# One gather for both rows of a pick: an expert layer whose two tables lie side by side

## The chip, the cores and the metric

The kernel runs on one core of a Trainium2 chip. The core has a matrix engine (PE; its weight loads are listed apart as PEld), a vector engine (DVE), a scalar engine (ACT), a general engine (POOL) and a queue engine (SP); 16 DMA engines bring data from the chip's memory (HBM) into the core's own (the tensor `arena`, 128 partitions), and matrix products end in a small memory of eight banks (`ps`). The metric is the device time of one execution in microseconds (us), as the median of several; less is better. Everything is in float32.

## What is computed

One layer of a decoder, for 512 prompt tokens and 8 sample tokens of 1024 numbers: retention and attention heads, cross-attention, and then the part that the change is about, a product-key expert layer (PEER). For each token and each of 8 heads it picks 16 of 16,384 experts, so 128 picks a token. An expert is one row `u` and one row `v`, of 1024 numbers (4 KB) each:

```
idx = jnp.take_along_axis(cand_i, best_pos, axis=-1)          # 8 heads x 16 picks a token
g = jax.nn.softmax(best_s, axis=-1)
u = peer_u[idx]
a = jax.nn.gelu(jnp.einsum('nd,nhkd->nhk', xb, u), approximate=False)
v = peer_v[idx]
return jnp.einsum('nhk,nhkd->nd', g * a, v)
```

So `u` is wanted first (a dot product with the token), then gelu and the weight, and then `v` (times the weight, summed over the picks).

## The kernel before

The 512 prompt tokens are four blocks of 128, one token to a partition; the 8 sample tokens are a fifth block. The program is written out for each engine, and semaphores order the engines among each other.

**Gathers.** POOL issues all gathers of expert rows, in a loop over a block's picks (lines 508 to 533). One gather (L505) brings, for one pick number, one row for each of 128 tokens: 128 rows of 4 KB, 512 KB. Picks go in chunks of 8 (`CHUNK`): eight gathers of `u`, then eight of `v`. Each slot of `arena` has a semaphore for its landing (`u_in0` to `u_in7`, `v_in0` to `v_in7`), and a gather waits until its slot has been consumed: `u_used` counts the dot products, `v_used` the weighted sums.

**Block 0** has no stretch of its own. While the other blocks go through mixing, cross-attention and routing, its picks are fitted in between that work on DVE, as "half-steps" at 32 places (`PLACES`, lines 398 to 404): an even half-step is eight dot products (L1100), an odd one the weights and eight weighted sums (L1109). At most places there is one half-step. Only eight slots of 4 KB are free then (`VSLOT`); the other eight (`WSLOT`) hold weight matrices. So `u` and `v` of a chunk take turns in the same eight slots: the gathers of `v` start one by one as the dot products free the slots, and the next chunk's `u` as the weighted sums free them. Between two half-steps stands what the stage asks of DVE, often one residual addition (L1089, listed as L810, the line of the helper).

**Blocks 1 to 3** follow one after the other, with eight slots for `u` (`WSLOT`) and eight for `v` (`VSLOT`). For a chunk, DVE makes eight dot products (L1317), ACT the gelu of eight numbers (L776), DVE the eight weights (L1358; L1338 in block 1), ACT eight diagonal matrices of the weights (L780), and PE multiplies each with the slot of `v` and sums in `ps` (L1786). Between the chunks DVE selects the picks of the next block (`select_head`, lines 1139 to 1184). The gathers of block b + 1 wait on `sel_ready`, which DVE raises after the last head's selection (`gates`, line 1195); block 1's wait for each head's selection instead.

**The sample** comes last: eight gathers of `u`, eight of `v` (lines 535 to 540), one token each, with 128 picks on the partitions.

## Time and profile before

| | before |
|---|---|
| time, median of 3 runs | 2610.83 us (2597.9 to 2616.35) |
| the profiled execution: span, first to last instruction | 2647.7 us |
| PE / DVE / ACT / POOL busy | 73% / 59% / 14% / 47% |
| DMA over the whole span | 273 GB/s |
| gathers of expert rows (L505) | 520 of `peer_u`, 520 of `peer_v` |
| software-issued DMA (the gathers): share of 16 engines' span | 62.9% |
| HBM read | 713.11 MB |

The profiled execution's span is 36.9 us (1.4%) above the median of the unprofiled runs; no time of it other than its span is given. In the rows below, a timeline row gives start, duration, engine, line, operation, output and input, count, and in brackets how long the engine was idle before it and what ended that. A busy time by itself doesn't tell what limits a stage: one has to see which wait ends last there.

### The profile page before, as it was taken

Reading aid. Unit: us, or ns where it says so; the run is one execution under the profiler, and the core shown is the slowest. Engines: PE = TensorE matmul, PEld = TensorE weight load, DVE = VectorE, ACT = ScalarE, POOL = GpSimd, SP = SyncE. Lnnn points to the kernel's source line nnn. Section 1 sums busy time; section 2 is a strip of 40 time slices with the busy share of each in tenths; the row PEclk is TensorE's granted clock in tenths of the full one; section 3 lists DMA queues with packets and bytes.
Section 4 is the critical chain, followed back from the end, with each engine's and each line's share of the span. In section 5 each row is a group of like instructions: output and inputs, shape, how many; then the busy total and the mean of one; then the engine's idle time right before and its main releaser. Section 6 shows DMA issues by size and latency. Waiting matters only on the chain.

```text
span 2647.7 us, 19720 instructions
## 1 busy us (share of the span) xinstructions
PE 1938.7 (73%) x4940; PEld 856.2 (32%) x4940; DVE 1566.2 (59%) x3287; ACT 379.2 (14%) x859; POOL 1239.5 (47%) x1180
## 2 busy tenths in 40 slices
PE   5998798689876594478585667676767775667667
PEld 3334333522354133113352222232323232223222
DVE  1662367530148766977798667665655656555462
ACT  3012300000110012000200111111111112111111
POOL 0110001122001765457743777776777776777662
PEclk8999789599888897588897888887888887887886
DMA  6463034367442977788883999998999998999994
GB/s 266 172 253 115 32 120 162 131 250 255 167 141 103 359 288 315 246 340 309 302 301 115 362 358 346 369 361 326 359 368 358 364 367 315 359 367 354 354 347 159
DMA packets 207497, 723.91 MB, mean 273 GB/s; under 512 B 20009, under 2 KB 24873, under 8 KB 197073
## 3 DMA queue, kind: packets, MB, share of 16 engines
q0 software_dynamic: 159616, 614.54, 62.9%
q1 hardware_dynamic: 39632, 99.73, 10.3%
q10 hardware_dynamic: 8192, 8.95, 1.0%
q8 instruction: 28, 0.46, 0.1%
q14 instruction: 29, 0.23, 0.0%
HBM read 713.11 MB, written 10.03 MB: 273 GB/s over the span
## 4 chain that ended last, share of the span: by engine, by line
PE 30%; DVE 21%; issue 21%; POOL 14%; DMA 8%; ACT 3%; another core or an unknown queue 1%; POOLq 1%; DVEq 0%; ACTq 0%; SPq 0%
POOL arena L505 14%; PE ps L1435 11%; PE ps L1786 7%; DVE arena L810 5%; PE ps L1604 4%; DMA arena<-in_peer_u,arena 4%; DVE arena L1100 4%; DVE arena L1109 4%; DMA arena<-in_peer_v,arena 3%; DVE arena L1317 1%; PE ps L1398 1%; PE ps L1799 1%; DVE arena L1123 1%; DVE arena L1118 1%
## 5 line engine op out<-in xcount | busy, mean ns | idle before, releaser
L1786 PE MATMUL ps<-arena 128*128 128x512 f32 x1536 | 781.1, 672 | 361.0 <-ACT arena L780 208.5
L505 POOL DMA_INDIRECT arena<-in_peer_u,arena x520 | 581.3, 1118 | 284.5 <-issue 156.4
L505 POOL DMA_INDIRECT arena<-in_peer_v,arena x520 | 571.4, 1099 | 255.9 <-issue 144.2
L1317 DVE CUSTOM_DVE_ANT_0 arena<-arena 128x1024 f32<-128x1024 f32 x384 | 468.8, 1226 | 325.0 <-DMA arena<-in_peer_u,arena 292.4
L1786 PEld LDWEIGHTS ps<-arena 128*128 128x128 f32 x1536 | 328.2, 217 | 814.6 <-issue 580.2
L1435 PE MATMUL ps<-arena 128*128 128x512 f32 (+1 forms) x1168 | 534.7, 616 | 18.5 <-DVE arena L810 12.9
L1435 PEld LDWEIGHTS ps<-arena 128*128 128x128 f32 (+1 forms) x1168 | 205.2, 179 | 336.8 <-issue 334.5
L496 POOL DMA_INDIRECT arena<-in_cache_diff_k,arena x32 | 30.1, 941 | 421.4 <-DVE arena L873 366.5
L1109 DVE SCALAR_TENSOR_TENSOR arena<-arena 128x1024 f32<-128x1024 f32 x128 | 164.5, 1285 | 35.6 <-DMA arena<-in_peer_v,arena 26.1
L810 DVE TENSOR_TENSOR arena<-arena 128x256 f32<-128x256 f32 (+10 forms) x353 | 131.2, 396 | 77.4 <-remote 23.9
L810 DVE TENSOR_TENSOR arena<-arena,ps 128x2048 f32<-128x2048 f32 (+3 forms) x78 | 118.3, 1522 | 84.7 <-PE ps L1435 34.3
L1100 DVE CUSTOM_DVE_ANT_0 arena<-arena 128x1024 f32<-128x1024 f32 x128 | 151.5, 1225 | 19.6 <-DMA arena<-in_peer_u,arena 17.6
L1759 PE MATMUL ps<-arena 128*128 128x128 f32 (+1 forms) x512 | 132.1, 418 | 1.5 <-DVE arena L1278 0.8
L776 ACT ACTIVATE arena<-arena 128x8 f32<-128x8 f32 x48 | 10.1, 210 | 844.1 <-DVE arena L1317 567.1
L517 POOL COPY arena<-arena 128x8 uint32 x64 | 16.8, 262 | 237.9 <-DVE arena L810 201.4
L780 ACT ACTIVATE arena<-arena 128x128 f32<-128x128 f32 x384 | 117.4, 388 | 58.2 <-DVE arena L810 26.5
L810 DVE TENSOR_TENSOR arena<-ps,arena 128x512 f32<-128x512 f32 (+3 forms) x44 | 35.4, 827 | 148.1 <-PE ps L1607 104.9
L1604 PE MATMUL ps<-arena 128*8 128x512 f32 x256 | 111.9, 592 | 3.9 <-DMA arena<-in_cache_diff_v,arena 3.9
L1398 PE MATMUL ps<-arena 128*128 128x128 f32 (+1 forms) x256 | 41.1, 322 | 92.6 <-DVE arena L819 80.3
L1759 PEld LDWEIGHTS ps<-arena 128*128 128x128 f32 x512 | 86.9, 215 | 40.3 <-issue 9.1
L496 POOL DMA_INDIRECT arena<-in_cache_diff_v,arena x32 | 33.8, 1055 | 123.3 <-PE ps L1604 114.4
L580 ACT ACTIVATE arena<-ps 128x512 f32<-128x512 f32 (+1 forms) x43 | 25.6, 596 | 349.0 <-PE ps L1435 342.6
(227 smaller groups left out, 1437.9 us busy)
## 6 DMA issues: line engine op xcount, KB each, us to landing
arena<-in_w_pq SPq DMA_DIRECT2D x8, 2048.0 KB, 12.1
arena<-in_w_in SPq DMA_DIRECT2D x7, 2048.0 KB, 10.0
arena<-in_peer_u,arena POOLq DMA_INDIRECT x520
arena<-in_peer_v,arena POOLq DMA_INDIRECT x520
arena<-in_w_out SPq DMA_DIRECT2D x4, 2048.0 KB, 8.3
arena<-in_w_mq SPq DMA_DIRECT2D x4, 2048.0 KB, 16.0
arena<-in_w_mo SPq DMA_DIRECT2D x4, 2048.0 KB, 13.2
arena<-in_cache_mem_k SPq DMA_DIRECT2D x8, 1024.0 KB, 4.9
```

The source lines that it names most:

```text
L496: pool.indirect_dma_start(SLOT[n % RING], None, k_rows if kind == "k" else v_rows, bass.IndirectOffsetOnAxis(kv_idx[:, b * GRP + g:b * GRP ...
L505: return pool.indirect_dma_start(slot, None, table[0], bass.IndirectOffsetOnAxis(idx.bitcast(U32), 0))
L780: act.activation(DIAG[k], ident, ACT.Copy, scale=WCH[:, k:k + 1]).then_inc(s["diag_ready"], 1)
L810: return dve.tensor_tensor(out, a, b, op)
L1100: dve.tensor_tensor_reduce(VSLOT[k], VSLOT[k], QR[:, 0, :], 1.0, 0.0, ALU.mult, ALU.add, dots[:, k:k + 1]).then_inc(s["u_used"], 1)
L1109: dve.scalar_tensor_tensor(out=HR[:, 0, :], in0=VSLOT[k], scalar=WCH[:, k:k + 1], in1=HR[:, 0, :], op0=ALU.mult, op1=ALU.add).then_inc(s[" ...
L1317: dve.tensor_tensor_reduce(WSLOT[k], WSLOT[k], QR[:, blk, :], 1.0, 0.0, ALU.mult, ALU.add, dots[:, k:k + 1]).then_inc(s["u_used"], 1)
L1398: last = pe.transpose(tb[:, P * k:P * k + r], c, ident[0:r, 0:r])
L1435: last = pe.matmul(PS[0:r, PSUM_JOB + j % 2, :], xt[:, k, P * u:P * u + r], W[t % 2][:, k, :], start=(k == 0), stop=(k == KD - 1))
L1604: last = pe.matmul(PS[0:HC, 4 + b % 2, :], S[:, c0:c0 + HC], SLOT[n % RING][:, 512 * j:512 * j + 512], start=(g == 0 and j == 0), stop=False)
L1759: last = pe.matmul(PS[:, 4 + x % 2, 0:tokens], W[t % 2][:, k, P * (x % 4):P * (x % 4) + P], XT[:, k, first:first + tokens], start=(k == 0) ...
L1786: last = pe.matmul(PS[:, bank + i, :], DIAG[k], VSLOT[k][:, 512 * i:512 * i + 512], start=False, stop=False, skip_group_check=True)
```

## The change

The two tables arrive as one, `peer_uv`, whose row is an expert's `u` followed by its `v` (8 KB). The joining is done once on the host and is no part of the device time. One gather of 128 rows of 8 KB brings both rows of a pick, and a slot is 8 KB: four slots (`UV0`) while block 0 runs, in the same 32 KB a partition that the eight slots took, and eight (`UV`) from block 1 on, in the same 64 KB. A slot is free again only when its `v` half has been used, so every gather waits on `v_used`. 

In block 0 a batch is four picks. Each place has twice as many half-steps as before: where there was one (eight dot products, or eight weighted sums) there are now both halves of one batch: four dot products, gelu, weights, four weighted sums. In blocks 1 to 3 dot products, gelu, weights and diagonals go in pairs of picks (`PAIR`): DVE makes the dot products of pair q, then the weights of pair q - 1. The region `misc` is moved to the front of the layout so that a slot of 8 KB fits across two neighbouring regions.

```diff
-CHUNK = 8
+UV0 = 4
+UV = 8
+PAIR = 2
...
-        VSLOT = ([at("const", CO["rot"][0] + 1024 * i, 1024) for i in range(3)] + [at("xtm", 1024 * i, 1024) for i in range(2)]
-                 + [at("dvs", 0, 1024)] + [at("ring", 4096 + 1024 * i, 1024) for i in range(2)])
-        WSLOT = [at("w", 1024 * i, 1024) for i in range(CHUNK)]
+        UVSLOT = ([at("const", CO["rot"][0] + NB * NSEL + 2048 * i, 2048) for i in range(2)] + [at("xtm", 0, 2048), at("ring", 4096, 2048)]
+                  + [at("w", 2048 * i, 2048) for i in range(UV - UV0)])
+        USLOT, VSLOT = [x[:, 0:D] for x in UVSLOT], [x[:, D:2 * D] for x in UVSLOT]
...
         def half_steps_at(place):
-            before = sum(n for i, (p, n) in enumerate(PLACES) if i < [q for q, _ in PLACES].index(place))
-            return range(before, before + dict(PLACES)[place])
+            before = 2 * sum(n for i, (p, n) in enumerate(PLACES) if i < [q for q, _ in PLACES].index(place))
+            return range(before, before + 2 * dict(PLACES)[place])
...
-                        for k in range(CHUNK):
-
-                            pool.wait_ge(s["u_used"] if blk else s["v_used"], c2 * (2 * CHUNK) + (done + k + 1))
+                        for k in range(UV):
+
+                            pool.wait_ge(s["v_used"], c2 * (2 * UV) + free_count(blk, UV * half + k))
                             pool.nop(nofuse=True)
-                            gather(uslot[k], peer_u, ICH[half][:, k:k + 1]).then_inc(uv_in[0][k], 16)
-                        for k in range(CHUNK):
-
-                            if blk:
-                                pool.wait_ge(s["v_used"], c2 * (2 * CHUNK) + (done + k + 1))
-                            else:
-                                pool.wait_ge(s["u_used"], c2 * (2 * CHUNK) + (done + CHUNK + k + 1))
-                            pool.nop(nofuse=True)
-                            gather(VSLOT[k], peer_v, ICH[half][:, k:k + 1]).then_inc(uv_in[1][k], 16)
+                            slot = k if blk else k % UV0
+                            gather(UVSLOT[slot], ICH[half][:, k:k + 1]).then_inc(uv_in[slot], 16)
...
+            def turn_of_slots(blk, c):
+                for q in range(UV // PAIR):
+                    ks = range(PAIR * q, PAIR * q + PAIR)
+                    act.wait_ge(s["u_used"], c * UV + dotted(blk, ks[-1]))
+                    act.activation(gl[:, ks[0]:ks[-1] + 1], dots[:, ks[0]:ks[-1] + 1], ACT.Gelu).then_inc(s["gelu_done"], 1)
+                    act.wait_ge(s["weight_ready"], c * (UV // PAIR) + (NBATCH + NSEL // PAIR * (blk - 1) + q + 1))
+                    for k in ks:
+                        act.wait_ge(s["v_used"], c * UV + free_count(blk, k))
+                        act.activation(DIAG[k], ident, ACT.Copy, scale=WCH[:, k:k + 1]).then_inc(s["diag_ready"], 1)
...
-                        for k in range(CHUNK):
-                            dve.wait_ge(uv_in[1][k], 16 * (c + 1))
-                            dve.wait_ge(s["v_used"], CHUNK * (c + 1) + k)
+                        for k in range(UV0):
+                            dve.wait_ge(s["v_used"], UV0 * (c + 1) + k)
                             dve.scalar_tensor_tensor(out=HR[:, 0, :], in0=VSLOT[k], scalar=WCH[:, k:k + 1], in1=HR[:, 0, :],
                                                      op0=ALU.mult, op1=ALU.add).then_inc(s["v_used"], 1)
...
-            def weights_wanted(blk, c, h2):
-                dve.wait_ge(s["gelu_done"], h2 * 2 + (NCH * blk + c + 1))
-                dve.wait_ge(s["v_used"], h2 * (2 * CHUNK) + CHUNK * (NCH * blk + c + 1))
+            def weights_wanted(blk, half, h, q):
+                dve.wait_ge(s["gelu_done"], h * (2 * UV // PAIR) + (NBATCH + NSEL // PAIR * (blk - 1) + UV // PAIR * half + q + 1))
+
+
+            def picks(blk, half, h, weigh):
+
+                for q in range(UV // PAIR):
+                    dot_products(blk, half, h, q)
+                    if q:
+                        weigh(half, q - 1)
+                weigh(half, UV // PAIR - 1)
...
+    inputs["peer_uv"] = np.concatenate([np.asarray(inputs.pop(name)) for name in ("peer_u", "peer_v")], axis=2)
```

Where the instructions stand. First DVE in block 0, at the first two places (the mixing stage's residual additions are the rows with `job_ready`). Before, from the last dot product of one place to the first weighted sums of the next:

```order
L1100 ISA arena<-arena 128x1024 [waits u_in7]
L1100 ISA arena 128x1
L810 TENSOR_TENSOR arena<-arena,ps 128x512 [waits job_ready]
L810 TENSOR_TENSOR arena<-arena,ps 8x512 [waits job_ready]
L810 TENSOR_TENSOR arena<-arena 128x8 [waits gelu_done]
L1109 SCALAR_TENSOR_TENSOR arena<-arena 128x1024 [waits v_used,v_in0,weight_ready]
L1109 SCALAR_TENSOR_TENSOR arena<-arena 128x1024 [waits v_used,v_in1]
```

and now, from the last dot product of a batch to the first of the next batch:

```order
L1104 ISA arena<-arena 128x1024 [waits uv_in3]
L1104 ISA arena 128x1
L814 TENSOR_TENSOR arena<-arena 128x4 [waits gelu_done]
L1112 SCALAR_TENSOR_TENSOR arena<-arena 128x1024 [waits v_used,weight_ready]
L1112 SCALAR_TENSOR_TENSOR arena<-arena 128x1024 [waits v_used] x3
L814 TENSOR_TENSOR arena<-arena,ps 128x512 [waits job_ready]
L814 TENSOR_TENSOR arena<-arena,ps 8x512 [waits job_ready]
L1104 ISA arena<-arena 128x1024 [waits uv_in0]
```

The residual additions stood between the dot products and the weighted sums of a chunk; now they stand between two batches, and the weights follow the dot products at once.

Second POOL, at the turn from one chunk to the next in block 0. Before:

```order
L517 COPY arena<-arena 128x8
L519 REGISTER_ALU
L505 DMA arena<-in_peer_u,arena 128x1024 [waits idx_copied,v_used]
L505 DMA arena<-in_peer_u,arena 128x1024 [waits v_used] x7
L531 REGISTER_ALU
L505 DMA arena<-in_peer_v,arena 128x1024 [waits u_used]
```

and now:

```order
L530 COPY arena<-arena 128x8
L532 REGISTER_ALU
L535 REGISTER_ALU [waits idx_copied]
L519 DMA arena<-in_peer_uv,arena 128x2048 [waits v_used]
L535 REGISTER_ALU
```

The gathers of `v`, which waited for dot products, are gone, and each gather that is left brings twice the bytes and waits for a weighted sum.

Third DVE in the loop of blocks 2 and 3. Before, the end of one chunk and the start of the next:

```order
L1317 ISA arena<-arena 128x1024 [waits u_in7]
L1317 ISA arena 128x1
L1321 ISA
L1322 ISA [waits gelu_done]
L810 ISA [waits v_used]
L810 TENSOR_TENSOR arena<-arena 128x8
L1316 REGISTER_ALU
L1317 ISA arena<-arena 128x1024 [waits u_in0]
```

and now, the end of a turn of eight slots and the start of the next:

```order
L1319 ISA arena<-arena 128x1024 [waits uv_in7]
L1319 ISA arena 128x1
L1323 REGISTER_ALU
L814 ISA [waits gelu_done]
L814 TENSOR_TENSOR arena<-arena 128x2
L1323 REGISTER_ALU
L814 ISA [waits gelu_done]
L814 TENSOR_TENSOR arena<-arena 128x2
```

The wait on `v_used` ahead of the weights is gone; two weight instructions, of the last two pairs, follow the last dot product.

## Rows read from the trace of the kernel before

**Rows 1.** Stages: start:end, us, busy by engine, PEclk, DMA share, GB/s

```profile
851.00:1421.00 570.00, 404.19 (x1119) 184.40 (x1119) 439.84 (x763) 63.07 (x127) 333.59 (x272) 0.81 0.81 297
1444.00:1823.00 379.00, 251.75 (x495) 106.09 (x496) 255.91 (x626) 66.57 (x176) 276.17 (x272) 0.81 0.95 354
1823.00:2198.00 375.00, 266.92 (x518) 111.80 (x517) 219.74 (x514) 64.59 (x162) 273.04 (x272) 0.82 0.96 358
2198.00:2590.00 392.00, 266.10 (x536) 112.06 (x534) 225.07 (x533) 69.54 (x170) 271.42 (x271) 0.83 0.93 344
```

**Rows 2.** DVE's groups from 851 to 1421 us: count, busy us, mean ns

```profile
L1109 DVE SCALAR_TENSOR_TENSOR arena<-arena 128x1024 f32<-128x1024 f32 x128 | 164.5, 1285 | 35.6 <-DMA arena<-in_peer_v,arena 26.1 <-DVE arena L1109 0.5
L1100 DVE CUSTOM_DVE_ANT_0 arena<-arena 128x1024 f32<-128x1024 f32 x128 | 151.5, 1225 | 19.6 <-DMA arena<-in_peer_u,arena 17.6 <-ACT arena L563 1.1
```

**Rows 3.** DVE's timeline in block 0, four neighbouring half-steps

```profile
1210.73 11.01 DVE L1109 SCALAR_TENSOR_TENSOR arena<-arena 128x1024 f32<-128x1024 f32 x8
1221.66 0.68 DVE L810 TENSOR_TENSOR arena<-arena,ps 128x512 f32<-128x512 f32 x1
1222.26 1.22 DVE L1100 CUSTOM_DVE_ANT_0 arena<-arena 128x1024 f32<-128x1024 f32 x1
...
1231.42 1.27 DVE L810 TENSOR_TENSOR arena<-arena,ps 128x512 f32<-128x512 f32 x2
```

**Rows 4.** DVE's timeline, the end of a long gap before weighted sums

```profile
1035.48 0.18 DVE L1227 RECIPROCAL arena<-arena 128x4 f32<-128x4 f32 x1 [8.84 <-PE ps L1672]
...
1037.03 1.28 DVE L1109 SCALAR_TENSOR_TENSOR arena<-arena 128x1024 f32<-128x1024 f32 x1
```

**Rows 5.** POOL's timeline at those half-steps: gathers, and what ended the wait

```profile
1212.79 1.45 POOL L505 DMA_INDIRECT arena<-in_peer_u,arena  x1 [7.92 <-DVE arena L1109]
...
1226.88 1.99 POOL L505 DMA_INDIRECT arena<-in_peer_v,arena  x1 [0.31 <-issue]
```

**Rows 6.** The first gather of block 0 (POOL), and its first dot product (DVE)

```profile
852.33 0.96 POOL L505 DMA_INDIRECT arena<-in_peer_u,arena  x1 [0.87 <-POOL arena L517]
...
856.69 1.23 DVE L1100 CUSTOM_DVE_ANT_0 arena<-arena 128x1024 f32<-128x1024 f32 x1 [4.48 <-DMA arena<-in_peer_u,arena]
```

**Rows 7.** Timeline in block 2: gelu after the last dot product, weights

```profile
2003.30 0.21 ACT L776 ACTIVATE arena<-arena 128x8 f32<-128x8 f32 x1 [15.77 <-DVE arena L1317]
2003.74 0.60 DVE L810 TENSOR_TENSOR arena<-arena 128x8 f32<-128x8 f32 x2 [0.48 <-issue]
```

**Rows 8.** SP's queue of weights and memory rows, 851 to 1421 us: packets, MB, share

```profile
q1 hardware_dynamic: 10912, 34.60, 16.1%
```

**Rows 9.** Gather queue, 4 KB rows, 2250 to 2500 us

```profile
q0 software_dynamic: 24830, 90.43, 97.0%
```

**Rows 10.** Gather queue, 8 KB rows of the paged cache, 555 to 600 us

```profile
q0 software_dynamic: 1546, 11.29, 64.9%
```

**Rows 11.** The same gathers, 500 to 650 us

```profile
q0 software_dynamic: 4208, 30.02, 55.3%
```

**Rows 12.** Block 1's end: DVE's last weights, then POOL's next gather

```profile
1813.78 0.23 DVE L1338 SCALAR_TENSOR_TENSOR arena<-arena 128x8 f32<-128x8 f32 x1 [4.02 <-remote]
...
1823.54 0.96 POOL L505 DMA_INDIRECT arena<-in_peer_u,arena  x1 [0.86 <-POOL arena L517]
```

**Rows 13.** Block 3's end: DVE's last dot product, then POOL's sample gather

```profile
2569.31 1.23 DVE L1317 CUSTOM_DVE_ANT_0 arena<-arena 128x1024 f32<-128x1024 f32 x1
...
2590.43 0.94 POOL L505 DMA_INDIRECT arena<-in_peer_u,arena  x1 [15.36 <-DVE arena L1374]
```

**Rows 14.** Stretches at the three block ends, and one in block 0

```profile
1815.00:1826.00 11.00, 11.00 (x22) 4.57 (x22) 9.97 (x49) 4.44 (x9) 2.46 (x4) 0.82 0.33 109
2194.00:2206.00 12.00, 12.00 (x29) 5.34 (x28) 10.93 (x60) 1.59 (x2) 5.84 (x8) 0.98 0.62 217
2574.00:2592.00 18.00, 13.79 (x33) 5.87 (x32) 10.30 (x27) 7.57 (x11) 2.20 (x3) 0.96 0.47 189
1246.00:1250.00 4.00, 0.26 (x1) 0.00 (x0) 2.53 (x3) 0.00 (x0) 3.39 (x3) 0.88 1.02 408
```

More of the change, by code:

```diff
@@ L501, in _, with gather @@
                                    state_ret[0, b].rearrange("h d e -> d h e")).then_inc(tile_in[n % RING], 16)
-            def gather(slot, table, idx):
-                return pool.indirect_dma_start(slot, None, table[0], bass.IndirectOffsetOnAxis(idx.bitcast(U32), 0))
+            def gather(slot, idx):
+                return pool.indirect_dma_start(slot, None, peer_uv[0], bass.IndirectOffsetOnAxis(idx.bitcast(U32), 0))
             for blk in range(NBLK):
@@ L691, in peer_half_steps @@
                     if n % 2:
-                        act.wait_ge(s["u_used"], CHUNK * (n // 2 + 2))
-                        act.activation(gl, dots, ACT.Gelu).then_inc(s["gelu_done"], 1)
+                        act.wait_ge(s["u_used"], dotted(0, UV0 * (n // 2) + UV0 - 1))
+                        act.activation(gl[:, 0:UV0], dots[:, 0:UV0], ACT.Gelu).then_inc(s["gelu_done"], 1)
             def keep_sample_scores(x):
@@ L771, in _ @@
                     gate_exp(0)
-            def chunk(blk, c):
-                act.wait_ge(s["u_used"], c * CHUNK + CHUNK * (NCH * blk + 2))
-                act.activation(gl, dots, ACT.Gelu).then_inc(s["gelu_done"], 1)
-                act.wait_ge(s["weight_ready"], c + (NCH * blk + 1))
-                for k in range(CHUNK):
-                    act.wait_ge(s["v_used"], c * CHUNK + (CHUNK * NCH * blk + k + 1))
-                    act.activation(DIAG[k], ident, ACT.Copy, scale=WCH[:, k:k + 1]).then_inc(s["diag_ready"], 1)
+            def turn_of_slots(blk, c):
[7 more added lines that the diff above has]
+                        act.activation(DIAG[k], ident, ACT.Copy, scale=WCH[:, k:k + 1]).then_inc(s["diag_ready"], 1)
             with act.Fori(0, PH) as h:
@@ L785, in _ @@
                 for half in range(2):
-                    chunk(1, h * 2 + half)
+                    turn_of_slots(1, h * 2 + half)
             gate_exp(2)
             for blk in range(2, NBLK):
-                with act.Fori(0, NCH) as c:
-                    chunk(blk, c)
+                with act.Fori(0, NTURN) as c:
+                    turn_of_slots(blk, c)
                 gate_exp(blk + 1)
@@ L1333, in head_of_block_1, with weigh @@
                 dve.nop(nofuse=True)
-                for half in range(2):
-                    if half:
-                        dot_products(1, 1, h)
-                    weights_wanted(1, half, h)
-                    dve.scalar_tensor_tensor(out=WCH, in0=GE[:, CHUNK * half:CHUNK * half + CHUNK], scalar=rgate, in1=gl,
-                                             op0=ALU.mult, op1=ALU.mult).then_inc(s["weight_ready"], 1)
-                    if half == 0 and not last:
-                        select_head(1, 1, h + 1)
+                def weigh(half, q):
+                    weights_wanted(1, half, h, q)
+                    dve.scalar_tensor_tensor(out=WCH[:, PAIR * q:PAIR * q + PAIR], in0=GE[:, UV * half + PAIR * q:UV * half + PAIR * q + PAIR],
+                                             scalar=rgate, in1=gl[:, PAIR * q:PAIR * q + PAIR], op0=ALU.mult, op1=ALU.mult
+                                             ).then_inc(s["weight_ready"], 1)
+                picks(1, 0, h, weigh)
+                if not last:
+                    select_head(1, 1, h + 1)
+                picks(1, 1, h, weigh)
                 select_head(2, 2, h)
@@ L1354, in _, with weigh @@
                 with dve.Fori(0, PH) as h:
-                    for half in range(NCH // PH):
-                        dot_products(blk, half, h)
-                        weights_wanted(blk, half, h)
-                        tt(WCH, gl, GATE[:, blk, bass.ds(h * (2 * CHUNK) + half * CHUNK, CHUNK)], ALU.mult).then_inc(s["weight_ready"], 1)
+                    def weigh(half, q):
+                        weights_wanted(blk, half, h, q)
+                        tt(WCH[:, PAIR * q:PAIR * q + PAIR], gl[:, PAIR * q:PAIR * q + PAIR],
+                           GATE[:, blk, bass.ds(h * (2 * UV) + half * UV + PAIR * q, PAIR)], ALU.mult).then_inc(s["weight_ready"], 1)
+                    for half in range(2):
+                        picks(blk, half, h, weigh)
                     select_head(blk + 1, blk + 1, h)
@@ L1780, in _ @@
                 open_group(bank, P)
[L1781 to L1784 removed]
+                with pe.Fori(0, NTURN) as c:
+                    for k in range(UV):
+                        pe.wait_ge(s["diag_ready"], c * UV + (NSEL * (blk - 1) + k + 1))
                         for i in range(2):
@@ L1801, in _ @@
                 last.then_inc(s["xb_ready"], 1)
[L1802 removed]
+            pe.wait_ge(s["u_used"], dotted(NBLK, DB - 1))
             open_group(6, DB)
```

90 lines of the change are left out of this document (41 added, 49 removed).

## The prediction, made before the changed kernel was run

> **What bounds the kernel now.** I read the stages first [rows 1]. In blocks 1 to 3 the DMA engines are busy 0.93 to 0.96 of the time and no engine more than 0.73: these 1146 us are bound by the gathers. Block 1's 379 us less 7.4 us idle at its end [rows 14] make 2.90 us for each of 128 picks, 1.05 MB at about 362 GB/s, as in [rows 9].
>
> Block 0's stage (851 to 1421 us) is different. DVE is the busiest (440 of 570 us), DMA has 0.81 [rows 1]. DVE's groups say what it does: 164.5 us of weighted sums and 151.5 us of dot products, and it waits only 26.1 and 17.6 us for their rows [rows 2]. The timeline shows why so little: eight weighted sums take 11.0 us without a stop, 0.6 us of other work, then the dot products run at once [rows 3], because the gather of the next `u` began at 1212.79, right after the first weighted sum had freed its slot [rows 5]. Consuming and loading overlap over a whole half-step. From the same timeline I took the 31 gaps between the 32 half-steps, from the end of one to the start of the next (two are in [rows 3], 0.6 and 1.3 us; a long one ends in [rows 4]). 19 are under 7 us, 32 us together; 12 are 7.8 to 32 us, 167 us together.
>
> **Block 0: the loads come out from under the work.** A batch is now four picks; pick j waits for the weighted sum of pick j - 4, and weighted sums are the last thing in a batch. So during the dot products, gelu and weights nothing is loading. From the end of a batch's first weighted sum:
> - the gather starts 0.8 us later (1212.0 to 1212.79) [rows 3, 5];
> - its rows are in 4.4 us after that (852.33 to 856.69) for 512 KB [rows 6], and the second 512 KB add 1.4 us at 362 GB/s;
> - the other three picks follow at 2.9 us each: 8.7 us.
>
> So the fourth pick is in after 15.3 us. The other three weighted sums take 4.1 us (1.38 each [rows 3]), so this is 11.2 us after the batch's end. The dot products alone would reach the fourth 3.5 us after they start (1.15 each: eight in 1222.26 to 1231.42 [rows 3]). A gap g thus leaves a wait of 7.7 us - g. The 19 short gaps cost 19 x 7.7 - 32 = 114 us, the long ones nothing. (One round of a tight run then takes 18 to 19 us, where a half-step and its gap now take about 12.)
>
> Second, gelu and weights now stand inside the batch: gelu starts at 2003.30, the weights end at 2003.91, and the next work starts about 0.2 us later, 0.85 us in all [rows 7]. 32 times this, less the 16 weight instructions of 0.2 us that the gaps held: +24 us.
>
> Third, the 44 us of waits that DVE has now [rows 2] are replaced by these: -44 us.
>
> Fourth, the chain was costed with free DMA engines, but SP moves 34.6 MB in this stage [rows 8], 95 us at that rate. Between nothing and 95 x 19/31 = 58 us of it falls into exposed loads; I take the middle, +30.
>
> Fifth, some gaps are waits for PE or ACT (8.84 us in [rows 4]) that were started before the batch ahead of them; a longer batch uses them up. Three such gaps follow a lengthened batch (5 to 6 us each), and at one place dot products can go ahead of a late gelu: between 0 and -35 us, I take -20.
>
> Sum for block 0: 114 + 24 - 44 + 30 - 20 = +104; I take **+100**, between +40 (all ends in its favour, and a chain 1 us shorter) and +150.
>
> The gathers in this stage become fewer, and under running dot products one takes 1.99 us instead of 0.96 [rows 5, 6]. That is no gain here: POOL mostly waits for DVE.
>
> **Blocks 1 to 3: the ends.** The last eight `v` of a block, 11.6 us of DMA, stream in while DVE already does the last weights, the selection and `gates`; only then may the next gather start. So DMA now idles only 7.4, 4.6 and 9.5 us at the three ends (the missing part of the DMA share in the first three of [rows 14]). With `u` and `v` together, the last dot product comes after the last byte. At block 1's end the weights start at 1813.78, after 4.0 us on `v_used` that fall away, and the next gather at 1823.54: 9.8 us [rows 12]. To this come 1.2 us of dot product, about 1.8 us for the weights of the last two pairs and the diagonals between them (gelu 0.85 us as above), and about 2.8 us from gather to data and from landing to DVE (between nothing and the 2.9 us that [rows 6] leave beside the transfer): 15.6 us. Twice this, and for the third end 2570.5 to 2590.43 [rows 13] + 1.3 + 1.2 + 2.8 = 25 us, are 56 us against 21.5: **+35** (27 to 45).
>
> **Blocks 1 to 3: the rate.** Between the ends the gathers bound the time before and, I expect, after. Eight slots of 8 KB hold as much as sixteen of 4 KB. A slot is held while its pair is dotted, the next pair lands and is dotted (5.8 us), then 0.85 us, two diagonals and two products of PE, some 12 us; the round of eight is 23.2 us, and a refill takes 0.8 + 5.8 us. It fits, with about 5 us to spare. What remains is how fast rows of 8 KB go. With 4 KB the queue moves 90.43 MB in 0.970 of 250 us: 373 GB/s while busy [rows 9]. The trace has 8 KB rows too, in the gathers of the paged cache: 387 in a dense stretch [rows 10], 362 in a looser one [rows 11]. For 1114 us these are -40 and +34 us. The dense stretch is nearer to this use, but it shares the engines with SP's queue; I take **-15**.
>
> The Trainium skill ("DMA: Bandwidth & Descriptors", section "Anatomy of one DMA") fits a software-issued DMA as 2.0 us plus bytes at 436 GB/s, so 512 KB would take 3.2 us and 1 MB 4.4 us, an estimate by that page. If gathers went one at a time, a pick would fall from 6.4 to 4.4 us, and the sum would be hundreds of us lower. The trace disagrees with that use of it: two gathers pass in 2.90 us, less than one would take, so the fixed part is already overlapped.
>
> **The sample.** The first pair of rows is in 1.4 us later; after that PE's broadcasts set the pace as before: **+1.5**. Half of POOL's gathers fall away and buy nothing there: POOL is busy 0.73 of blocks 1 to 3 [rows 1], and runs ahead of the DMA engines. The smaller gelus and weights there cost ACT and DVE under 1 us a pair, beside 5.8 us of DMA.
>
> **Sum.** 100 + 35 - 15 + 1.5 = +121.5 us on the profiled 2647.7 us, or 4.6%. The median is 2610.83 us, so I scale by 0.986: +120, **2731 us**.
>
> **Rivals.**
> - *A, not slower: one read of 8 KB goes at the rate that the queue shows only at its best.* 408 GB/s stands in [rows 14] (1246 to 1250 us). If 8 KB rows kept that, 396 with the present 0.97 share, blocks 1 to 3 would lose 96 us, and four picks of block 0 would be in 1.1 us earlier, 19 times: 100 - 21 + 35 - 96 + 1.5 = +20, 2630 us. For: the dense stretch is above 373. Against: [rows 11]. It decides from about 395 GB/s on. 12%. The Trainium skill's page on DMA points this way in its section "Measured": its rates rise with a DMA's size, 341 GB/s at 1 MB and 425 at 16 MB.
> - *B, slower still: the slots starve the DMA queue in blocks 1 to 3.* The spare 5 us must cover a selection (most of the 9.8 us in [rows 12], some 7 us), in which DVE dots nothing. If each of the 31 selections (15 in block 1, 8 each after) left DMA idle for 2 us: +62, 2792 us. For: a slot now returns only through PE. Against: weights and diagonals of the last pair are out before the selection starts, so all eight slots fill during it. 15%.
> - *C: block 0 hides most of it.* If the stage's length is set by PE and ACT more than DVE's gaps show, block 0 costs +40: 2672 us. For: DVE idles 130 of 570 us [rows 1], and 86 of these are not for expert rows. Against: the short gaps hold residual additions of 0.7 us, with nothing behind them. 20%.
>
> My forecast has 53%. For it alone I would say 2690 to 2775 us. 2640 to 2800 us also takes in most of B and C and leaves out the better part of A and the far end of B. About 1% (26 us) is what can be told from no change: faster by more than that 3% (A at its best), within it 9% (the rest of A, a little of C), slower 88%.
>
> **What would show it.** In the changed profile: (1) block 0's stage some 100 us longer, its dot products waiting for `peer_uv` about 120 to 150 us in all where 17.6 us stood, the weighted sums waiting for no rows, and a DMA share near 0.7. (2) Gaps of 15 and 25 us without DMA at the three block ends. (3) Stretches inside blocks 2 and 3 at 0.96 or more DMA share and 355 to 375 GB/s; over 390 is A, a share under 0.93 is B. (4) POOL's busy time halved. If (1) fails, the chain of 15.3 us is wrong, most likely its 4.4 us, which was taken once, or the gaps are not DVE's own.

## The result, and the profile after

The changed kernel takes **2736.3 us** (median of four, 2728.4 to 2740.0) against 2607.8 us of the kernel before (2597.9 to 2616.4): a ratio of **1.0485, 95% interval 1.046 to 1.0509**. It is slower, and the predicted 2731 us is 5 us away. Where single executions of a kernel below were disturbed (3004 and 3290 us, in two kernels), they are left out of its median.

The stages of the changed kernel, as in [rows 1]: after the stretch and its length come the busy us of PE, PEld, DVE, ACT and POOL, PE's granted clock as a share of full speed, the DMA share and GB/s (here block 0's stage runs up to the first gather of block 1):

```profile
851.00:1549.00 698.00, 427.59 (x1139) 194.67 (x1139) 468.17 (x896) 68.52 (x148) 141.33 (x145) 0.76 0.63 242
1549.00:1923.00 374.00, 264.23 (x516) 109.42 (x516) 257.27 (x679) 76.81 (x226) 143.63 (x145) 0.84 0.90 359
1923.00:2292.00 369.00, 261.34 (x512) 107.90 (x512) 219.61 (x559) 74.34 (x210) 142.39 (x144) 0.85 0.91 364
2292.00:2669.00 377.00, 269.20 (x518) 110.58 (x518) 225.70 (x582) 79.27 (x218) 143.77 (x143) 0.84 0.90 358
```

Block 0 grew and its DMA share fell to 0.63. Blocks 1 to 3 seem to be 26 us shorter than in [rows 1], yet at a DMA share of only 0.90. That comparison misleads: the profiled execution of before was 40 us above its median. A second profile of the kernel before (the first experiment) is the better base. From first gather to first gather on POOL's timeline, in us:

| stage | before, first profile | before, second profile | after | after against the second |
|---|---|---|---|---|
| up to block 0's first gather | 852.3 | 860.0 | 852.0 | -8.0 |
| block 0 | 591.9 | 591.3 | 697.8 | **+106.5** |
| blocks 1, 2, 3 | 379.3, 375.0, 391.9 | 365.1, 361.2, 375.1 | 373.2, 369.7, 376.7 | **+18.2** |
| sample and end | 57.3 | 57.8 | 57.2 | -0.6 |

The first stage is not touched by the change and lies between 852 and 865 us in all the profiles here. From block 0's first gather on, the change costs 124 us; the sum predicted 121.5.

**Block 0.** DVE's waits in its stage (total, times, longest), to be read beside [rows 2]:

```profile
DVE arena L1104 <- DMA arena<-in_peer_uv,arena: 141.9, 79, 5.9
DVE arena L1230 <- PE ps L1687: 20.5, 3, 9.7
DVE arena L1119 <- PE ps L1764: 13.1, 9, 2.4
...
DVE arena L814 <- ACT arena L695: 8.7, 32, 0.3
```

The dot products wait 141.9 us for rows; the weighted sums (L1112) wait for none, as their group's row shows (after the last bar, 4.6 us of idle time, with no row among its causes):

```profile
L1112 DVE SCALAR_TENSOR_TENSOR arena<-arena 128x1024 f32<-128x1024 f32 x128 | 164.5, 1285 | 4.6
```

Before it was 17.6 + 26.1. One tight round, DVE first and then POOL:

```profile
1239.91 5.25 DVE L1112 SCALAR_TENSOR_TENSOR arena<-arena 128x1024 f32<-128x1024 f32 x4
1245.07 2.33 DVE L814 TENSOR_TENSOR arena<-ps,arena 4x1024 f32<-4x1024 f32 x2
1248.11 1.23 DVE L1104 CUSTOM_DVE_ANT_0 arena<-arena 128x1024 f32<-128x1024 f32 x1 [0.70 <-DMA arena<-in_peer_uv,arena]
...
1251.62 1.23 DVE L1104 CUSTOM_DVE_ANT_0 arena<-arena 128x1024 f32<-128x1024 f32 x1 [2.28 <-DMA arena<-in_peer_uv,arena]
...
1256.60 1.23 DVE L1104 CUSTOM_DVE_ANT_0 arena<-arena 128x1024 f32<-128x1024 f32 x1 [1.25 <-DMA arena<-in_peer_uv,arena]
...
1258.11 0.17 DVE L814 TENSOR_TENSOR arena<-arena 128x4 f32<-128x4 f32 x1 [0.27 <-ACT arena L695]
1258.31 5.25 DVE L1112 SCALAR_TENSOR_TENSOR arena<-arena 128x1024 f32<-128x1024 f32 x4
```

```profile
1241.97 1.38 POOL L519 DMA_INDIRECT arena<-in_peer_uv,arena  x1 [12.63 <-DVE arena L1112]
```

The first weighted sum ends at about 1241.2 (a quarter of 5.25 us). The gather follows 0.8 us later, its rows are dotted at 1248.11, the fourth pick's at 1256.60, 15.4 us after that first weighted sum. From weighted sums to weighted sums it is 18.4 us. The chain of 15.3 us and the round of 18 to 19 us of the prediction stand here row by row. It is not one lucky round: in 16 of the 31 the fourth dot product starts 14.9 to 15.8 us after the first weighted sum's end, in the others later, and the ten batches behind a gap of 8.7 us or more wait for no row.

**Blocks 1 to 3.** Cut at the block ends: three long stretches and the three ends of the changed kernel, then the same of the second profile of before.

```profile
1550.00:1906.00 356.00, 249.36 (x484) 103.33 (x485) 244.97 (x634) 70.73 (x213) 143.21 (x143) 0.83 0.94 373
1906.00:1928.00 22.00, 14.87 (x33) 6.08 (x31) 16.99 (x76) 5.14 (x11) 3.97 (x6) 0.89 0.31 117
1928.00:2276.00 348.00, 249.38 (x486) 103.13 (x487) 203.87 (x492) 69.20 (x199) 138.42 (x139) 0.84 0.95 380
2276.00:2298.00 22.00, 15.35 (x32) 5.74 (x30) 16.74 (x72) 5.14 (x11) 4.31 (x6) 0.92 0.28 102
2298.00:2645.00 347.00, 254.19 (x487) 104.94 (x488) 204.87 (x506) 69.98 (x202) 139.64 (x139) 0.84 0.96 382
2645.00:2670.00 25.00, 12.44 (x29) 5.16 (x28) 15.09 (x42) 9.29 (x16) 0.60 (x1) 0.83 0.15 63
```

```profile
1452.00:1804.00 352.00, 246.04 (x480) 103.11 (x480) 247.45 (x591) 60.06 (x164) 267.06 (x267) 0.82 0.99 371
1804.00:1820.00 16.00, 12.61 (x24) 5.43 (x25) 14.40 (x64) 5.53 (x12) 7.46 (x8) 0.73 0.69 267
1820.00:2170.00 350.00, 248.34 (x497) 104.41 (x496) 210.81 (x466) 61.68 (x159) 264.66 (x268) 0.86 0.99 377
2170.00:2182.00 12.00, 12.00 (x28) 5.33 (x27) 10.59 (x51) 2.92 (x4) 3.80 (x6) 0.96 0.59 213
2182.00:2530.00 348.00, 248.49 (x488) 104.08 (x486) 206.44 (x464) 59.06 (x150) 262.29 (x263) 0.83 0.99 372
2530.00:2556.00 26.00, 20.54 (x39) 8.72 (x40) 14.94 (x41) 10.47 (x20) 8.50 (x9) 0.82 0.61 226
```

Three things can be worked out (second last column: DMA share, last: GB/s).
- *Ends.* Without DMA: 0.69 x 22 + 0.72 x 22 + 0.85 x 25 = 52 us, against 0.31 x 16 + 0.41 x 12 + 0.39 x 26 = 20 us: **+32**.
- *Idle inside.* 0.06 x 356 + 0.05 x 348 + 0.04 x 347 = 53 us, against 0.01 x 1050 = 10 us: **+42**.
- *Rate while busy.* 373/0.94 = 397, 400 and 398 GB/s, against 375, 381 and 376. 384 picks of 1.049 MB are 403 MB; at 398 instead of 377 GB/s: **-57**.

The sum is +17, where +18.2 was measured. So a faster row was paid back almost in full by a queue that runs dry. Where it does is seen in block 2 after a selection. Windows, then PE and POOL:

```profile
2064.00:2068.00 4.00, 2.53 (x6) 0.76 (x4) 3.18 (x9) 0.00 (x0) 2.43 (x3) 1.00 1.00 422
2068.00:2072.00 4.00, 0.00 (x0) 0.00 (x0) 4.00 (x7) 0.21 (x1) 0.73 (x2) 0.89 1.01 426
2072.00:2076.00 4.00, 3.23 (x4) 1.51 (x5) 2.65 (x8) 0.79 (x3) 0.00 (x0) 0.50 1.01 422
2076.00:2078.00 2.00, 2.00 (x3) 0.67 (x2) 0.89 (x1) 0.79 (x3) 0.67 (x1) 0.51 0.83 344
2078.00:2080.00 2.00, 2.00 (x6) 0.95 (x5) 0.76 (x3) 0.00 (x0) 1.37 (x2) 1.00 0.35 82
```

```profile
2059.38 7.15 PE L1800 MATMUL ps<-arena 128*128 128x512 f32 x16 [0.51 <-ACT arena L784]
2072.77 13.56 PE L1800 MATMUL ps<-arena 128*128 128x512 f32 x25 [6.24 <-ACT arena L784]
```

```profile
2067.31 0.94 POOL L519 DMA_INDIRECT arena<-in_peer_uv,arena  x1 [0.79 <-PE ps L1800]
2068.24 0.49 POOL L530 COPY arena<-arena 128x8 uint32 x1
2077.33 1.84 POOL L519 DMA_INDIRECT arena<-in_peer_uv,arena  x1 [8.60 <-PE ps L1800]
```

During the selection (until 2067 us) DVE makes no weights, and the first pair's come only behind the second pair's dot products. ACT has no diagonals to make, PE nothing to do for 6.24 us, and then its granted clock is 0.50 (the level of 1.2 GHz) until 2078. The four products that free the first slot then start 0.85 us apart, at the full clock 0.43, so of the 8.6 us that POOL waits some 1.7 are the clock's (an estimate from those starts). POOL waits for a slot from 2068.7 to 2077.3, the gathers under way run out, and between 2078 and 2080 the DMA share is 0.35.

### The profile page after: what moved, and what is told of

Same layout as the page of the kernel before. It is cut to its first block, busy times and chain, and to the rows that moved or that the text cites. A ratio compares the mean times of both kernels' runs of the same rounds, so it can differ in the third digit from the quotient of the medians.

```text
span 2726.6 us, 19130 instructions
## 1 busy us (share of the span) xinstructions
PE 1963.2 (72%) x4940; PEld 859.0 (32%) x4940; DVE 1576.0 (58%) x3447; ACT 412.4 (15%) x1021; POOL 648.9 (24%) x660
## 4 chain that ended last, share of the span: by engine, by line
PE 39%; DMA 22%; DVE 21%; issue 12%; ACT 3%; POOL 3%; DVEq 1%; POOLq 0%; ACTq 0%; SPq 0%
DMA arena<-in_peer_uv,arena 20%; PE ps L1450 13%; PE ps L1800 12%; DVE arena L814 4%; PE ps L1619 4%; DVE arena L1319 3%; DVE arena L1104 3%; POOL arena L519 2%; PE ps L1774 2%; DVE arena L1112 2%; ACT arena L784 1%; PE ps L1764 1%; DVE arena L1181 1%; PE ps L1813 1%; PE ps L1687 1%
## 5 line engine op out<-in xcount | busy, mean ns | idle before, releaser
L1800 PE MATMUL ps<-arena 128*128 128x512 f32 x1536 | 789.4, 675 | 313.2 <-ACT arena L784 313.1
L519 POOL DMA_INDIRECT arena<-in_peer_uv,arena x520 | 557.3, 1072 | 1161.7 <-PE ps L1800 558.1
L1450 PEld LDWEIGHTS ps<-arena 128*128 128x128 f32 (+1 forms) x1168 | 206.0, 180 | 358.7 <-issue 356.0
L1104 DVE CUSTOM_DVE_ANT_0 arena<-arena 128x1024 f32<-128x1024 f32 x128 | 154.1, 1223 | 143.0 <-DMA arena<-in_peer_uv,arena 141.9
L784 ACT ACTIVATE arena<-arena 128x128 f32<-128x128 f32 x384 | 133.2, 394 | 548.5 <-DVE arena L814 353.5
L814 DVE TENSOR_TENSOR arena<-arena 128x256 f32<-128x256 f32 (+11 forms) x465 | 148.9, 339 | 57.3 <-ACT arena L780 33.3
L1112 DVE SCALAR_TENSOR_TENSOR arena<-arena 128x1024 f32<-128x1024 f32 x128 | 164.5, 1285 | 4.6
L1413 PEld LDWEIGHTS ps<-arena 128*128 128x128 f32 (+1 forms) x256 | 35.8, 178 | 158.1 <-DVE arena L823 83.4
L695 ACT ACTIVATE arena<-arena 128x4 f32<-128x4 f32 x32 | 6.6, 207 | 494.9 <-DVE arena L1104 494.9
L780 ACT ACTIVATE arena<-arena 128x2 f32<-128x2 f32 x192 | 37.0, 193 | 281.2 <-DVE arena L1319 281.2
```

What stands on the lines that cost most here:

```text
L519: return pool.indirect_dma_start(slot, None, peer_uv[0], bass.IndirectOffsetOnAxis(idx.bitcast(U32), 0))
L780: act.activation(gl[:, ks[0]:ks[-1] + 1], dots[:, ks[0]:ks[-1] + 1], ACT.Gelu).then_inc(s["gelu_done"], 1)
L784: act.activation(DIAG[k], ident, ACT.Copy, scale=WCH[:, k:k + 1]).then_inc(s["diag_ready"], 1)
L814: return dve.tensor_tensor(out, a, b, op)
L1104: dve.tensor_tensor_reduce(USLOT[k], USLOT[k], QR[:, 0, :], 1.0, 0.0, ALU.mult, ALU.add, dots[:, k:k + 1]).then_inc(s["u_used"], 1)
L1112: dve.scalar_tensor_tensor(out=HR[:, 0, :], in0=VSLOT[k], scalar=WCH[:, k:k + 1], in1=HR[:, 0, :], op0=ALU.mult, op1=ALU.add).then_inc(s[" ...
```

## The experiments

### Which base: the kernel before, profiled again (e8_before_again)

Expected: 

> The kernel before, unchanged, for a second profile of it: the first had a span of 2647.7 us, 40 us above its own median of 2606. If that execution was only an unlucky one, this span is about 2604 us, and the 40 us are missing in blocks 1 to 3 (first gather to first gather 379, 375, 392 us then, in sum 1146), which come to about 1105 us in sum, while block 0 stays at 592 us. Rival: the profiled execution always carries about 40 us more, spread over all stages; then the span is about 2645 us again.

Measured: span 2610.5 us, time 2612.4. Block 0 591.3 us, blocks 1 to 3 1101.4 us. The 45 us were missing in blocks 1 to 3 alone, as the first expectation had it. Inside the blocks the gathers moved 362 GB/s at a share of 0.97 in the first profile [rows 9], and 371 to 377 at 0.99 in the second (above). Why one execution's gathers were slower is open.

### Block 0 as it was (e1_block0_4k)

```diff
+        HSLOT = [UVSLOT[k // 2][:, D * (k % 2):D * (k % 2) + D] for k in range(UV)]
...
+                        if blk == 0:
+                            for table, used in ((peer_u, s["v_used"]), (peer_v, s["u_used"])):
+                                for k in range(UV):
+                                    pool.wait_ge(used, c2 * (2 * UV) + (UV * half + k + 1))
+                                    pool.nop(nofuse=True)
+                                    gather(HSLOT[k], ICH[half][:, k:k + 1], table).then_inc(uv_in[k], 16)
+                            continue
```

Expected: 

> The changed kernel, but block 0 as it was before: eight slots of 4 KB, eight gathers of u and eight of v in turns (from the two separate tables), half-steps of eight. Blocks 1 to 3 and the sample keep the 8 KB rows. Theory (in block 0 the loads come out from under the work): the loss sits in block 0 alone, so the stage from its first gather to block 1's first gather falls back from 698 to about 592 us and the time from 2736 to 2580 to 2630 us, not slower than the kernel before (2608). Rival (8 KB rows, pairs or the block ends cost it): block 0 gives back less than 50 us and the time stays above 2680.

Measured: 2627.4 us, ratio 1.0086 (1.0061 to 1.0112). Block 0 is back at 591.2 us, as expected, and blocks 1 to 3 stay at 1121 us; but the kernel is still 0.9% slower than the one before, which I had not expected. Of the 128 us that the change costs, 109 lie in block 0; what it does elsewhere costs the remaining 20 us.

### Batches of two (e2_batch2)

```diff
-                        for k in range(UV0):
-                            dve.wait_ge(uv_in[k], 16 * (c + 1))
...
+                    for k0 in range(0, UV0, SUB):
+                        for k in range(k0, k0 + SUB):
+                            dot(k)
+                        weigh_and_add(k0)
```

Expected: 

> The changed kernel with batches of two picks instead of four in block 0; same four slots, same gathers, same bytes. Theory (the chain from a freed slot to landed rows is exposed because all four slots are freed at the end of a batch): while one pair is worked on the other two slots load. From the end of a pair's first weighted sum its rows are in after 0.8 + 4.4 + 1.4 = 6.6 us and 9.5 us, and DVE comes back to them after 7.0 and 8.2 us, so about 1.3 us of wait is left for a pair. The dot products' wait for peer_uv falls from 142 us to 45 to 70 us, 32 more gelus and weights cost 15 us, time 2640 to 2690 us. Rival (the rows of 8 KB or the shared DMA engines limit block 0): same bytes, so the wait stays near 140 us and the time rises to about 2750.

Measured: 2694.3 us, ratio 1.0345 (1.0297 to 1.0393). DVE's waits in block 0:

```profile
DVE arena L1109 <- DMA arena<-in_peer_uv,arena: 52.6, 32, 5.9
DVE arena L817 <- ACT arena L698: 28.8, 64, 6.6
DVE arena L1131 <- PE ps L1776: 28.5, 9, 4.2
```

The same rows into the same slots, and the wait for them falls from 141.9 to 52.6 us. So most of that wait is neither the rows' size nor the shared engines, it is the batch that frees all slots at once. The time is 4 us above the expected range, because part came back: 20 us at gelu, and 15 us more at L1131, the router's top-16, which waits for PE's scores.

### A chain of single picks (e5_pipe)

```diff
...
+                    dot(0)
+                    for k in range(UV0):
+                        if k + 1 < UV0:
+                            dot(k + 1)
+                        weigh_and_add(k)
```

Expected: 

> The changed kernel with block 0's batches of four picks worked on in a chain of single picks: the dot product of pick k + 1 goes ahead of gelu, weight and weighted sum of pick k, so gelu is hidden behind a dot product and each slot is freed as soon as its pick is done. Same slots, gathers and bytes. Theory (exposed load chain plus inline gelu): after batches of two, 52.6 us of waits for rows and 28.8 us for gelu are left in block 0's stage (653 us). The gelu wait goes to nearly nothing, and a slot's refill (0.8 + 4.4 + 1.4 = 6.6 us) now has two dot products, two weights and two weighted sums (5.5 us) in front of it, so the wait for rows falls to 15 to 35 us; 64 more weights cost 13 us, and as with batches of two some 15 us come back as waits for PE: stage 605 to 630 us, time 2645 to 2675 us. Rival (what is left in block 0 is PE's and the shared DMA engines' time): the stage stays above 640 us and the time above 2680.

Measured: 2682.8 us, ratio 1.0272 (1.024 to 1.0305); block 0's stage 644.2 us. My expectation (stage 605 to 630 us, time 2645 to 2675) missed, and the rival's numbers came in. The gelu wait halved, but the wait for rows did not fall any more:

```profile
DVE arena L1109 <- DMA arena<-in_peer_uv,arena: 54.3, 40, 6.2
DVE arena L1132 <- PE ps L1777: 30.5, 9, 4.5
...
DVE arena L817 <- ACT arena L698: 14.1, 5, 6.6
```

What is left of this wait can be read gather by gather. Two gathers on POOL, and then the dot products of the same two picks:

```profile
1259.24 1.43 POOL L521 DMA_INDIRECT arena<-in_peer_uv,arena  x1 [2.55 <-DVE arena L1120]
1260.98 3.17 POOL L521 DMA_INDIRECT arena<-in_peer_uv,arena  x1 [0.30 <-issue]
```

```profile
1268.63 1.23 DVE L1109 CUSTOM_DVE_ANT_0 arena<-arena 128x1024 f32<-128x1024 f32 x1 [3.81 <-DMA arena<-in_peer_uv,arena]
1271.42 1.23 DVE L1109 CUSTOM_DVE_ANT_0 arena<-arena 128x1024 f32<-128x1024 f32 x1 [0.16 <-DMA arena<-in_peer_uv,arena]
```

The second gather takes 3.17 us, while DVE runs dot products and weighted sums without a stop, but its dot product waits only 0.16 us. The long wait, 3.81 us, is for the first gather: it began on time, 0.8 us after its slot came free, and its rows came 9.4 us later, while SP's queue was moving weights. Over the whole of block 0, the 81 gathers without traffic of SP's queue between issue and landing took 6.1 us (median), the 47 with it 8.7 us, and two thirds of DVE's waits for rows are for the latter. So most of what is left falls beside SP's transfers, as the rival had it; that they cause it is not shown, as no run here takes them away. The 30.5 us of waiting for PE could be followed too, and it is not PE's own time:

### The order on ACT (e11_act_order)

The waits of PE in the router's loop of the changed kernel, and then of this one:

```profile
PE ps L1764 <- ACT arena L766: 32.3, 6, 13.0
```

```profile
PE ps L1766 <- ACT arena L766: 16.4, 4, 12.3
```

In the changed kernel ACT's gelu of a batch (L695) stands ahead of its copy of the next router product (L766). One of the six places, ACT and then PE:

```profile
1426.40 0.21 ACT L695 ACTIVATE arena<-arena 128x4 f32<-128x4 f32 x1 [15.98 <-DVE arena L1104]
1426.51 0.47 ACT L766 COPY arena<-ps 128x392 f32<-128x392 f32 x1
```

```profile
1427.03 2.18 PE L1764 MATMUL ps<-arena 128*128 128x128 f32 x8 [3.87 <-ACT arena L766]
```

ACT stands 15.98 us until the batch's last dot product is done, the copy starts only behind the gelu, and PE stands 3.87 us for the copy.

```diff
-                    peer_half_steps(g, ("router", x))
+                    if x:
+                        peer_half_steps(g, ("router", x - 1))
+                peer_half_steps(g, ("router", NSUB - 1))
```

Expected: 

> The changed kernel with that edit alone (ACT's copy of the next router product ahead of the gelu of a batch). Theory: DVE's 13.1 us of waits for PE's router scores go and PE's 32.3 us of waits for ACT in the router's loop with them; block 0's stage 685 to 690 us instead of 698, time 2722 to 2730 us instead of 2736. Rival: no change, 2733 to 2740 us, the wait for PE's scores at 13 us as before.

Measured: 2719.9 us, ratio 1.0426 (1.0391 to 1.046), block 0's stage 688.0 us; 2 us below the expected range. DVE's wait for the router's scores falls from 13.1 to 1.2 us, while the wait for rows stays at 143.7 us. PE's wait for ACT, which was to go, fell only by half; 12.3 of the 16.4 us left are in the loop's first place. So 10 of block 0's 106 us (16 in the median) came from ACT's queue, which the prediction did not look at.

### Two gathers of 4 KB rows into a slot (e4_two_4k)

```diff
-                            gather(UVSLOT[slot], ICH[half][:, k:k + 1]).then_inc(uv_in[slot], 16)
+                            if blk:
+                                gather(USLOT[k], ICH[half][:, k:k + 1], peer_u).then_inc(uv_in[k], 16)
+                                gather(VSLOT[k], ICH[half][:, k:k + 1], peer_v).then_inc(uv_in[k], 16)
+                            else:
+                                gather(UVSLOT[slot], ICH[half][:, k:k + 1]).then_inc(uv_in[slot], 16)
```

Expected: 

> The changed kernel, but in blocks 1 to 3 a pick's two rows come by two gathers of 4 KB rows (from the two separate tables) into the two halves of the same slot; slots, pairs, waits and order stay. Theory (a row of 8 KB goes faster): while busy the queue falls from 403 to the 373 GB/s of before; with the same stalls that is 40 to 90 us over 384 picks, time 2775 to 2825 us. Rival (row size doesn't matter, and the higher rate comes from elsewhere): 2720 to 2750 us with 400 GB/s while busy.

Measured: 2800.1 us, ratio 1.0758 (1.0707 to 1.0808), 64 us above the changed kernel, all of it in blocks 1 to 3 (402, 386 and 399 us). The gather queue (packets, MB, share of 250 us), changed kernel from 2000 us and this one from 2030 us:

```profile
q0 software_dynamic: 13082, 95.25, 94.5%
```

```profile
q0 software_dynamic: 24837, 90.44, 96.7%
```

95.25 MB in 0.945 of 250 us are 403 GB/s while busy; 90.44 in 0.967 are 374. Slots, pairs and order are the same. The row's size differs, and with it the bytes of a gather (two of 512 KB for one of 1 MB) and the tables, two for one; these are not told apart in blocks 1 to 3 (in block 0, 4 KB rows from two tables or out of the joined one made no difference, e7 and e10 below). The gain from one gather of 8 KB rows is real, and larger than I had it. (The Trainium skill, "DMA: Bandwidth & Descriptors", section "Measured", gives rates that rise with a DMA's size; the direction agrees here, 374 GB/s for gathers of 512 KB and 403 for those of 1 MB, though both are above its 341 for 1 MB.)

### The selection in four parts (e3_split_select)

```diff
-                        picks(blk, half, h, weigh)
-                    select_head(blk + 1, blk + 1, h)
+                        picks(blk, half, h, weigh, () if half else select_parts(blk + 1, blk + 1, h))
...
                     dot_products(blk, half, h, q)
                     if q:
                         weigh(half, q - 1)
+                    next(parts, None)
```

Expected: 

> The changed kernel with each head's selection in blocks 1 to 3 cut into four parts, one behind each pair of picks, instead of in one piece of about 8 us between two turns; all else as it is. Theory S (during a selection PE runs out of weights, frees no slot for some 6 us and comes back at half its clock, so the DMA queue runs dry for about 3 us behind each of 31 selections): these gaps go, and at the three block ends the last selection no longer stands between the last dot product and the next gather (7.5 us each); blocks 1 to 3 lose 80 to 130 us, time 2610 to 2660 us, with a DMA share of 0.97 and more and over 390 GB/s inside the blocks. Rival (the gathers themselves go no faster than the 381 GB/s seen inside block 2): only the block ends are gained, 22 us, time 2714.

Measured: 2678.7 us, ratio 1.0296 (1.0229 to 1.0362). Block 2's inner stretch and its end:

```profile
1920.00:2248.00 328.00, 241.73 (x480) 98.30 (x480) 209.09 (x518) 68.56 (x197) 140.19 (x140) 0.89 0.99 400
2248.00:2267.00 19.00, 18.68 (x36) 7.78 (x36) 11.21 (x41) 5.79 (x14) 3.02 (x4) 0.83 0.42 160
```

The DMA share inside is 0.99, the rate 400 GB/s and more: the cause is the right one. The size was too high, and the time missed the expected range by 19 us. The idle inside was 53 us, not 31 x 3, and the ends gained 14 us (52 to 38), not 22. The cut takes away the late weights and PE's slow return together, so this run does not tell them apart.

### The same cut in the kernel before (e9_before_split)

The same four parts, one behind each second dot product of a chunk, in the kernel before.

Expected: 

> The kernel before (4 KB rows, separate u and v slots) with the same cut of each selection into four parts, one behind each second dot product. Theory (the cut helps only where a slot returns late through a pair's weights; before, the eight slots of v went on loading through a selection, so the DMA share inside the blocks was already 0.97): at most the block ends gain, time within 15 us of 2606 us. Rival (the selection starved the queue before as well): 2560 to 2580 us, and then the 8 KB rows of blocks 1 to 3 gain nothing beside it.

Measured: 2616.1 us, ratio 1.0026 (0.9994 to 1.0058). No gain: the kernel before keeps a DMA share of 0.99 through its selections as it is (second profile, above). The starving is the change's own.

### Put together (e7_b0_split, e10_joined_split, e6_pipe_split, e12_pipe_split_act)

Block 0 as before and the cut selection:

> Block 0 as before (eight slots of 4 KB, u and v in turns) together with the selection cut into four parts in blocks 1 to 3, which keep the 8 KB rows and the pairs. If the two places are independent, the gains add: 109 us (block 0 as before) and 57 us (cut selection) off 2736 give 2570 us, between 2560 and 2585, about 1.4% faster than the kernel before. Rival (the faster gathers of blocks 1 to 3 depend on what block 0 left): above 2600.

Measured: **2567.1 us, ratio 0.9837 (0.9806 to 0.9868)**, the gains add. It beats both kernels, but holds the tables twice. The next one has only the joined table and gathers 4 KB rows out of it in block 0:

```diff
+            halves = peer_uv[0].rearrange("e (t d) -> (e t) d", t=2)
...
+                    dve.tensor_scalar(IDX[0:r, b, bass.ds(h * TOPK, TOPK)].bitcast(U32), GAC[0:r, 0:TOPK], 2.0, None, ALU.mult)
```

> As block 0 of before with the cut selection, but with the joined table as the only table: block 0 gathers 4 KB rows out of it (DVE stores twice the expert's number for u, and one more for v), so that no table is held twice. Theory (what counts in block 0 is eight slots of 4 KB in turns, not which table they come from): 2567 us again, 2558 to 2582. Rival (4 KB rows that lie 8 KB apart come slower, or the second index copy on POOL delays block 0's gathers): 2590 us and more, with block 0's stage above 600 us.

Measured: 2569.8 us, ratio 0.9863 (0.9814 to 0.9911), block 0 586.4 us. The same gain with one table. Then one gather for every pick, in block 0 too, with e5's chain and the cut selection:

> One gather of 8 KB rows for every pick, in block 0 too: the chain of single picks in block 0 together with the cut selection in blocks 1 to 3. If the two gains add (54 us and 57 us off 2736): 2626 us, 2612 to 2640, still slower than the kernel before (2608) or equal to it, because block 0's stage stays at about 644 us. Rival (block 0's remaining 50 us came from what blocks 1 to 3 do at their start): under 2600 us.

Measured: 2623.6 us, ratio 1.005 (1.0028 to 1.0073), block 0 649.4 us, as expected. And with ACT's order changed as well:

> The chain of single picks in block 0 and the cut selection, and one more edit: in the router's loop ACT makes the copy of the next router product (x + 1) ahead of the gelus of place x. Theory (ACT takes its instructions in order, so a gelu that waits for a batch's last dot product holds the copy behind it, PE waits for that copy, 33 us in five places, its clock falls, and DVE waits 30.5 us for PE's scores): these waits fall to a few us, block 0's stage from 649 to 615 to 625 us, and the time from 2624 to 2590 to 2602 us, not slower than the kernel before, with one gather of 8 KB rows for every pick. Rival (PE is late for its own reasons): the stage stays within 8 us of 649 and the time above 2610.

Measured: 2598.7 us, ratio 0.996 (0.9942 to 0.9977), block 0 615.0 us; both as expected. With three repairs, one gather for every pick comes 0.4% below the kernel before; the 29 us that it lacks to the joined table with 4 KB rows in block 0 are block 0's, 615 against 586.

## Why the prediction was right, step by step

- **The chain in block 0: right, and for its reason.** 15.3 us predicted, 15.4 read. The load term was 114 - 44 + 30 = 100 us; DVE's waits for rows went from 43.7 to 141.9 us, +98. Batches of two take 89 of the 141.9 us away with the same bytes.
- **Inline gelu and weights (+24): wrong.** The price of 0.85 us was taken from blocks 2 and 3. In block 0 DVE waits 0.27 us for gelu, 8.7 us in all, and the long gelu waits of before (20.6 us) fell away: -12. DVE is also busy 7 us longer. Together -5.
- **Absorbed gaps (-20): wrong the other way.** DVE's other idle time did not shrink, it grew by some 12 us: the other waits in its list by 17, of which 13.1 are for the router scores that ACT's gelu held up (e11) and that DVE did not wait for before, and gaps too short for the list gave 5 back. I had named what waits behind the weights on DVE, and not what waits behind the gelu on ACT. The two errors nearly cancel: +4 predicted, +7 measured.
- **The block ends (+35): right.** 52 us against 20, +32. The single ends are 15.2, 15.8 and 21.3 us, where 15.6, 15.6 and 25 were said.
- **The rate (-15): right only as a sum.** It is -57 by the faster gathers and +42 by a queue that starves; that these come to -15 is luck. The rate of rival A nearly held while the queue was busy (397 to 403 GB/s, where A had 408 and was to decide from 395), and so did the starving of rival B (42 us, where it said 62). I had weighed them as two cases that exclude each other, and the forecast's number came out between them. The step that failed is "it fits, with about 5 us to spare": that reckoned a slot's round without a selection, and without PE's return at half its clock. That all eight slots fill during a selection was true, and no defence: full slots are what stops the queue.
- **The sample (+1.5): -0.6.** No change that can be told: sample and end take 55 to 59 us in all the profiles here.
- **What would show it.** (1) and (2) were seen, but for the DMA share in block 0 (0.63, not 0.7). (3) was missed: it called for 355 to 375 GB/s at a share of 0.96 or more in blocks 2 and 3, and these have 380 and 382 GB/s at 0.95 and 0.96, short of the signs named for A (over 390) and B (under 0.93), though both were at work. (4) POOL's busy time went from 47% to 24% of the span, and the time did not fall by it.
- **The scaling by 0.986** spread the profiled execution's excess over all stages. It lay in blocks 1 to 3 only (e8); the block 0 term needed no scaling. This moved the result by 2 us.
- **The number.** The two large terms, the exposed loads and the block ends, were right by their mechanism. That the sum came within 5 us of the time is in part luck: two pairs of errors cancelled, gelu against gaps and rate against starving.

## What to carry to other kernels

Merging two loads into one makes each buffer wait for its last reader. Before counting saved transfers, draw the chain from a freed buffer to the landed data, and see whether all buffers come free at the same moment; if so, smaller batches on the same buffers give part of it back (42 and 54 of 128 us here). Then walk every engine's own queue: what stands behind the instruction that now waits longer (here ACT's copy behind a gelu) is as much part of the price. And when two rivals do not exclude each other, price both together.

## What was not expected of the hardware

- Gathers of 8 KB rows ran at 397 to 405 GB/s while busy, gathers of 4 KB rows at 373 to 381 ([rows 9], e4, and the stretches above), in e4 into the same slots in the same order.
- Once PE had stood for 6.24 us, its first products came at a granted clock of 0.50 for 5 to 6 us; where the wait was cut (e3), block 2's inner stretch had 0.89 in the mean instead of 0.84.
- The same program's gathers differed by 45 us in 1146 between two executions, with the rest of the program equal to 1 us but for the start.
